# Keys times values ahead of the inverse, and the bonus as 64x64 products, in a chunked RWKV-7 scan

## The chip, the cores and the metric

The kernel runs on one core of one Trainium2 chip. The metric is device time in microseconds (us), the median of three executions. A separate execution was profiled; the traces below are of it. The whole program is two transformer blocks with mixture-of-experts layers and, in the second block, an RWKV-7 branch. The change touches only the scan of that branch.

## The reference, cut to what matters

Each of 8 heads holds a 64x64 state S. Going over the tokens (256 context tokens without output, then 1024 with output), forwards in one direction and backwards in a second, the reference does:

```python
def step(S, inp):
    r_t, w_t, kk_t, b_t, k_t, v_t = inp
    sa = jnp.einsum('bhvk,bhk->bhv', S, -kk_t)
    S = S * w_t[:, :, None, :] + sa[..., None] * b_t[:, :, None, :] + v_t[..., None] * k_t[:, :, None, :]
    y = jnp.einsum('bhvk,bhk->bhv', S, r_t) if emit else None
    return S, y
...
bonus = jnp.sum(r * k_sum * r_k.astype(jnp.float32), axis=-1, keepdims=True) * v
```

The kernel does this in chunks of 64 tokens. Within a chunk the dependence of each token on the ones before it becomes a triangular 64x64 matrix, whose inverse is built in five doublings. The state after a chunk is the decayed state before it, plus B^T times U (U is the solved correction), plus K^T times V (keys times values). The bonus is a sum over 64 channels for each token and head.

## The kernel before, in words

**Work units.** `scan` runs four independent streams: direction d (0, 1) times group g (0, 1) of four heads. Each stream goes over 10 tiles of 128 tokens, the first two of which are context tiles that emit nothing. A tile holds two chunks of 64 (cc = 0, 1), which occupy partition halves. There are 40 pieces of work (stream, tile); "a tile" below means one of them. Each stream has its own SBUF buffers (`b`), two PSUM banks (A and B = A + 1) and its own semaphores.

**Order.** Each engine has a generator per stream that issues a part of the tile's work and yields. `take_turns` starts a stream every `LAG = PHASES // 4` turns (25 // 4 = 6), and in each turn lets all live streams issue one phase, stream 0 first and stream 3 last. So the order in each engine's queue is fixed when the program is built, and is the same rotation on all engines. An engine works its queue strictly in that order. A tile has 25 phases.

The phases of a tile before the change, with the lines of the profile:

- 0: TensorE multiplies the decay and rate low-rank weights (L2387, "lora"); ScalarE takes four tanh (L2516) and one affine pass (L2519).
- 1: VectorE's running sum of the log decay (L2606); GpSimd scales the key (L2561). 2: L2610 on VectorE, L2565 on GpSimd; ScalarE's three exponentials (L2524 to L2526).
- 3: VectorE's block of five operations (L2616 to L2621) that ends with `scaled`.
- 4: TensorE's 16 "pairs" products (L2399), which wait for `scaled`; GpSimd's three products (L2569 to L2571).
- 5: VectorE masks the pairs (L2625, 128x1024). 6: TensorE turns two key tensors (L2410, 128x128 transposes) and forms L_k_v (L2415); ScalarE copies both out (L2530, L2533); VectorE starts the inverse (L2632 to L2636).
- 7 to 16: five levels of the inverse, two phases each: x (L2427, masked by VectorE L2642) and m (L2441, or L2443 in the last level; VectorE adds in L2654 and, but for the last level, turns in L2658).
- 17, 18, 19 for the first chunk and 20, 21, 22 for the second: a (L2456, then VectorE Z L2663), u (L2462, then ScalarE's copy L2540), s (L2471 and L2472, then VectorE's new state L2670). GpSimd forms the decayed state (L2581) at 17 and 20.
- 23: the state's part of y (L2482). 24: the rest of y (L2495, L2497) and the bonus (L2500), then VectorE adds the bonus (L2681) and copies or adds y (L2683, L2685), which releases the banks (`tile_done`) for the stream's next tile.

Each fp32 matmul has two records in the profile, a transpose one. So 8 matmuls are x16. Where a wait stands in the code: s forms both products into one PSUM region,

```python
pe.matmul(out, b.tm[C, 0, col:col + 64], b.U[C, slot(par, jj)], start=True, stop=False)
last = pe.matmul(out, b.tm[C, 1, col:col + 64], v_rows(C, t, slice(h * 64, h * 64 + 64)),
                 start=False, stop=True)
```

and the bonus takes two 128x128 weight loads for four columns each (L2500). All other matmuls of the scan but the transposes and lora are 64x64.

Of the kernel before, what the change touches and what calls it, by code (L numbers as in the profile page):

```python
# [19 lines left out]
ALU = mybir.AluOpType  # L20
ACT = mybir.ActivationFunctionType
# [22 lines left out]

PARTS = [(0, 0), (0, 1), (1, 0)]

PHASES = 25


class Stream:  # L50
# [1978 lines left out]
def rwkv(c, h, hc, w_in, conv, vT):  # L2029
# [205 lines left out]
    for n in range(4):  # L2235
        b = Stream()
        b.lw, b.rate, b.F, b.e1, b.e3, b.kd = (c.at(name, 6 + 8 * n + i, [P, 2, P]) for i, name in enumerate((
            "log_decay", "rate", "running_log", "exp_after", "exp_inverse", "key")))
        b.ar = c.at("a_and_r", 12 + 8 * n, [P, 2, 2, P])
        b.bt, b.kt, b.bb, b.kb, b.rk = b.rate, b.e3, b.lw, b.F, b.kd  # L2240
        H = 74 + 12.5 * n if n < 3 else 38
        b.LL = c.at("pairs", H, [P, 2, 2, 2, 2, 64])
        b.M = c.at("inverse", H + 4, [P, 4, 64])
        b.MT = c.at("inverse_turned", H + 5, [P, 4, 64])
        b.X = c.at("below_diagonal", H + 6, [P, 4, 32])
        b.XW = c.at("below_diagonal_wide", WIDE + n, [P, 4, 64])
        b.tm = c.at("b_and_k_rows", H + 6.5, [P, 2, 256])
        b.LKV = c.at("L_k_v", H + 8.5, [P, 4, 64])
        b.Z = c.at("a_state", H + 9.5, [P, 4, 64])
        b.U = b.LKV  # L2250
        b.S = c.at("state", H + 10.5, [P, 3, 2, 64])
        b.SG = c.at("state_decayed", H + 12, [P, 2, 64])
        b.ge = c.at("decay_to_end", 55.25 + n / 32, [P, 4])
        streams.append(b)
# [77 lines left out]
def scan(c, loads, tiles_of, streams, masks, rw, v_rows, y, sc, ka, half, rate_bias, rks, keep, eye, w2, DEC):  # L2332
# [15 lines left out]
    def first_blocks(a, level, d):  # L2348
# [7 lines left out]
    names = ("lora_done", "tanh_done", "log_ready", "running_ready", "exps_ready", "key_scaled", "key_ready", "scaled",  # L2356
             "ends_scaled", "pairs_done", "pairs_masked", "bk_turned", "bk_copied", "lkv_done", "lkv_copied",
             "mt_ready", "m_ready", "x_done", "x_masked", "x_wide_cleared", "m_done", "a_state_done", "z_ready",
             "u_done", "u_ready", "decayed", "s_done", "state_ready", "y_started", "y_done", "tile_done", "state_cleared")
    both = [f"{n}_{i}" for i in range(4) for n in names]  # L2360
    with stage(nc, "dve_step", "tables_loaded", *both) as (block, dve_step, tables_loaded, *sems):
        sem = [dict(zip(names, sems[i * len(names):(i + 1) * len(names)])) for i in range(4)]
# [10 lines left out]
        def _(pe):  # L2373
            pe.wait_ge(tables_loaded, 16 * len(loads))

            def stream(d, g, b, s, A):
                B = A + 1
                order = (0, 1) if d == 0 else (1, 0)
                for i, t in enumerate(tiles_of[d]):
# [38 lines left out]
                    last.then_inc(s["lkv_done"], 1)  # L2418
                    yield
                    pe.wait_ge(s["bk_copied"], i + 1)  # L2420
                    for level in range(5):
                        n = 5 * i + level
                        pe.wait_ge(s["m_ready"], n + 1)
                        for par, jj in HEADS:
                            h4 = slot(par, jj)
                            for cc, C in CH:
                                last = pe.matmul(ps[C, A, h4 * 32:(h4 + 1) * 32], b.LL[C, par, 0, jj, 0, :],  # L2427
                                                 first_blocks(b.M[C, h4], level, d), start=True, stop=True)
                        last.then_inc(s["x_done"], 1)
                        yield  # L2430
                        if n == 4:
                            pe.wait_ge(s["x_wide_cleared"], 1)
                        if level == 0:
                            pe.wait_ge(s["lkv_copied"], i + 1)
                        pe.wait_ge(s["x_masked"], n + 1)
                        pe.wait_ge(s["mt_ready"], n + i + 1)
                        for h4 in range(4):
                            for cc, C in CH:
                                out = ps[C, B, h4 * 32:(h4 + 1) * 32]
                                if level < 4:  # L2440
                                    last = pe.matmul(out, b.MT[C, h4], b.X[C, h4], start=True, stop=True)  # L2441
                                else:
                                    last = pe.matmul(out, b.XW[C, h4], b.MT[C, h4, second_half(d)],  # L2443
                                                     start=True, stop=True)
                        last.then_inc(s["m_done"], 1)
                        yield
# [3 lines left out]
                    for q, cc in enumerate(order):  # L2450
                        C, n = half_of(cc), 2 * i + q
                        if n:
                            pe.wait_ge(s["state_ready"], n)
                        for jj in (0, 1):
                            for par in (0, 1):
                                last = pe.matmul(ps[C, A + par, jj * 64:(jj + 1) * 64], b.ar[half_of(par), jj, 0, C],  # L2456
                                                 b.S[half_of(par), n % 3, jj], start=True, stop=True)
                        last.then_inc(s["a_state_done"], 1)
                        yield
                        pe.wait_ge(s["z_ready"], n + 1)  # L2460
                        for h4 in range(4):
                            last = pe.matmul(ps[C, A + cc, 256 + h4 * 64:256 + (h4 + 1) * 64], b.MT[C, h4], b.Z[C, h4],  # L2462
                                             start=True, stop=True)
                        last.then_inc(s["u_done"], 1)
                        yield
                        pe.wait_ge(s["u_ready"], n + 1)
                        for jj in (0, 1):
                            for par in (0, 1):
                                col, h = (2 * jj + par) * 64, 4 * g + 2 * jj + par
                                out = ps[half_of(par), A + cc, 256 + jj * 64:256 + (jj + 1) * 64]  # L2470
                                pe.matmul(out, b.tm[C, 0, col:col + 64], b.U[C, slot(par, jj)], start=True, stop=False)  # L2471
                                last = pe.matmul(out, b.tm[C, 1, col:col + 64], v_rows(C, t, slice(h * 64, h * 64 + 64)),  # L2472
                                                 start=False, stop=True)
                        last.then_inc(s["s_done"], 1)
                        yield
                    if emit:
                        pe.wait_ge(s["state_ready"], 2 * i + 2)
                        for q, cc in enumerate(order):
                            C = half_of(cc)
                            for jj in (0, 1):  # L2480
                                for par in (0, 1):
                                    last = pe.matmul(ps[C, A + par, 128 + jj * 64:128 + (jj + 1) * 64],  # L2482
                                                     b.ar[half_of(par), jj, 1, C],
                                                     b.S[half_of(par), (2 * i + q) % 3, jj],
                                                     start=(jj == 0), stop=False)
                        last.then_inc(s["y_started"], 1)
                    yield
                    if emit:
                        pe.wait_ge(s["y_started"], sum(1 for x in tiles_of[d][:i + 1] if x >= 2))
                        for jj in (0, 1):  # L2490
                            for par in (0, 1):
                                h = 4 * g + 2 * jj + par
                                for cc, C in CH:
                                    out = ps[C, A + par, 128 + jj * 64:128 + (jj + 1) * 64]
                                    pe.matmul(out, b.LL[C, par, 0, jj, 1, :], b.U[C, slot(par, jj)],  # L2495
                                              start=False, stop=False)
                                    pe.matmul(out, b.LL[C, par, 1, jj, 1, :], v_rows(C, t, slice(h * 64, h * 64 + 64)),  # L2497
                                              start=False, stop=(jj == 1))
                        for jj in (0, 1):
                            last = pe.matmul(ps[:, A, 384:388], b.rk[:, jj], rks[:, 2 * g + jj, 4 * g:4 * g + 4],  # L2500
                                             start=(jj == 0), stop=(jj == 1))
                        last.then_inc(s["y_done"], 1)
                    yield

# [3 lines left out]
        def _(act):  # L2508
            def stream(d, g, b, s, A):
                B = A + 1  # L2510
                for i, t in enumerate(tiles_of[d]):
# [19 lines left out]
                       .then_inc(s["bk_copied"], 1)  # L2531
                    act.wait_ge(s["lkv_done"], i + 1)
                    act.activation(flat(b.LKV), ps[:, B, 0:256], ACT.Copy, scale=-1.0).then_inc(s["lkv_copied"], 1)  # L2533
                    for _ in range(11):
                        yield
                    for q, cc in enumerate((0, 1) if d == 0 else (1, 0)):
# [13 lines left out]
        def _(pool):  # L2550
            def stream(d, g, b, s, A):
# [3 lines left out]
                for i, t in enumerate(tiles_of[d]):  # L2555
# [3 lines left out]
                    for jj in (0, 1):  # L2559
# [10 lines left out]
                    pool.tensor_tensor(halves(b.kb), halves(b.kt), end(b.ge[:]), ALU.mult)  # L2570
                    pool.tensor_tensor(b.rk[:], r_[:, 2 * g:2 * g + 2, tok(t)], b.kd[:], ALU.mult)\  # L2571
                        .then_inc(s["ends_scaled"], 1)
                    for _ in range(13):
                        yield
                    for q, cc in enumerate((0, 1) if d == 0 else (1, 0)):
                        ends = b.ge[:].rearrange("p (j q) -> p j q", q=2)[:, :, cc].unsqueeze(2)\
# [1 line left out]
                        n = 2 * i + q  # L2578
                        if n:
                            pool.wait_ge(s["state_ready"], n)  # L2580
                        pool.tensor_tensor(b.SG[:], b.S[:, n % 3], ends, ALU.mult).then_inc(s["decayed"], 1)  # L2581
                        yield
                        yield
                        yield
# [6 lines left out]
        def _(dve):  # L2591
# [3 lines left out]
            def stream(d, g, b, s, A):  # L2595
# [4 lines left out]
                for i, t in enumerate(tiles_of[d]):  # L2600
# [34 lines left out]
                    dve.wait_ge(s["mt_ready"], 6 * i + 1)  # L2635
                    dve.transpose(flat(b.M), flat(b.MT)).then_inc(s["m_ready"], 1)  # L2636
                    yield
                    for level in range(5):
                        n = 5 * i + level
                        dve.wait_ge(s["x_done"], n + 1)  # L2640
# [34 lines left out]
                    if emit:  # L2675
# [2 lines left out]
                        tile_y = ps[:, A:A + 2, 128:256].rearrange("p a (j e) -> p a j e", e=64)  # L2678
                        bonus = sc[:, row, 4 * g:4 * g + 4]
                        dve.wait_ge(s["y_done"], sum(1 for x in tiles_of[d][:i + 1] if x >= 2))  # L2680
                        step(dve.tensor_tensor(bonus, bonus, ps[:, A, 384:388], ALU.add))  # L2681
                        if i < tiles_of[1 - d].index(t):
                            dve.tensor_copy(out, tile_y).then_inc(s["tile_done"], 1)  # L2683
                        else:
# [119 lines left out]
```

## Time and profile before

| what | value |
|---|---|
| three runs | 4667.0, 4673.45, 4680.64 us (median 4673.45) |
| the profiled execution | 4685.91 us, of which the span of the trace is 4684.1 us |
| mean granted TensorE clock, whole span | 0.926 of full speed |
| the scan in the trace | 3112 to 3681 us from the span's start: 569 us |
| busy in the scan | TensorE 522.8, VectorE 430.1, ScalarE 163.7, GpSimd 184.6 us |

The scan is 12% of the time. The clock column gives the mean granted TensorE clock of a stretch: 1.00 is 2.4 GHz, 0.50 is 1.2 GHz. A timeline merges neighbouring instructions of one line into one row (start, time from first start to last end, count); a bracket gives idle time before it and the instruction that ended it. Durations of matmuls overlap, so the cost of a group is read from its start to the start of the next group.

### The profile page before, as it was taken

How to read it: one execution, taken by the hardware profiler on the slowest of the kernel's cores; microseconds unless marked ns; L12 is line 12 of the kernel's file. 1: busy time of each engine (PE TensorE's matmuls, PEld its weight loads, DVE VectorE, ACT ScalarE, POOL GpSimd, SP SyncE). 2: the span in 40 equal slices, each digit the busy share in tenths (PEclk: the TensorE clock that was granted, in tenths of full speed). 3: DMA queues.
4: the chain of work that ended last, by engine and by line, in shares of the span. 5: the costliest groups of instructions: out<-in, count | busy, mean ns of one | idle time of the engine just before them, and what ended most of it. 6: DMA issues, size and time to landing. Idle time of an engine off the chain costs nothing. (4 is left out here: it accounts for less than half of the span.)

```text
span 4684.1 us, 80619 instructions
## 1 busy us (share of the span) xinstructions
PE 4090.9 (87%) x33798; PEld 3351.7 (72%) x33798; DVE 2731.3 (58%) x4351; ACT 1734.2 (37%) x2825; POOL 331.2 (7%) x419
## 2 busy tenths in 40 slices
PE   6999986997898998699479877889999587999997
PEld 5878864886786667388367766768888466888886
DVE  2347736885675553688546102647787644556556
ACT  2136622774363442377537211223233112222222
POOL 0000000220000000022000000013333001000000
PEclk9999997998999999799789998978999698999998
DMA  2100027995000002799500112000000121111111
GB/s 101 45 10 2 2 107 274 376 392 193 19 2 1 1 1 78 290 371 397 206 20 2 55 63 72 28 13 3 3 4 3 61 109 63 36 54 37 54 46 41
DMA packets 139157, 425.54 MB, mean 91 GB/s; under 512 B 14661, under 2 KB 50381, under 8 KB 114221
## 3 DMA queue, kind: packets, MB, share of 16 engines
q1 hardware_dynamic: 129580, 386.83, 21.4%
q0 software_dynamic: 9216, 33.56, 2.8%
q8 instruction: 269, 4.41, 0.4%
q14 instruction: 92, 0.75, 0.1%
HBM read 370.03 MB, written 50.33 MB: 90 GB/s over the span
## 5 line engine op out<-in xcount | busy, mean ns | idle before, releaser
L557 PE MATMUL psum<-weight_parts,h_parts 128*128 128x512 f32 (+2 forms) x2880 | 601.5, 371 | 45.8 <-DVE weight_parts L703 29.4
L557 PEld LDWEIGHTS psum<-weight_parts,h_parts 128*128 128x128 f32 x2880 | 508.3, 192 | 133.1 <-DVE weight_parts L703 30.5
L1520 DVE TENSOR_TENSOR weight_parts<-weights_raw,weight_parts 128x2048 fp32r<-128x2048 f32 x192 | 431.6, 2288 | 57.2 <-ACT weight_parts L1490 56.4
L911 ACT ACTIVATE scores<-scores,softmax_stats 128x1024 f32<-128x1024 f32 (+2 forms) x288 | 307.9, 1069 | 331.5 <-DVE softmax_stats L956 331.4
L1490 ACT ACTIVATE weight_parts<-weights_raw 128x2048 fp32r<-128x2048 f32 x192 | 360.4, 1919 | 71.3 <-DMA weights_raw<-in_moe_w_up 42.2
L1428 PE MATMUL psum<-weight_parts,picked_parts 128*128 128x512 f32 x1536 | 364.6, 397 | 15.6 <-DVE weight_parts L1520 10.8
L1901 PE MATMUL psum<-h_parts,up_parts 128*128 128x512 f32 x1536 | 355.4, 393 | 11.0 <-DVE up_parts L1976 11.0
L1917 PE MATMUL psum<-down_parts,hidden_parts 128*128 128x512 f32 x1536 | 353.5, 391 | 6.7 <-DVE down_parts L1981 6.7
L703 DVE TENSOR_TENSOR weight_parts<-weights_raw,weight_parts 128x2048 fp32r<-128x2048 f32 (+2 forms) x48 | 100.7, 2098 | 428.2 <-ACT weight_parts L612 428.1
L1428 PEld LDWEIGHTS psum<-weight_parts,picked_parts 128*128 128x128 f32 x1536 | 291.1, 191 | 79.3 <-issue 11.5
L1901 PEld LDWEIGHTS psum<-h_parts,up_parts 128*128 128x128 f32 x1536 | 291.3, 190 | 72.8 <-DVE up_parts L1976 11.8
L1917 PEld LDWEIGHTS psum<-down_parts,hidden_parts 128*128 128x128 f32 x1536 | 290.1, 189 | 67.7 <-DVE down_parts L1981 7.1
L868 PE MATMUL psum<-identity,scores 128*128 128x128 f32 x2096 | 277.4, 281 | 4.9 <-ACT probs_turned L920 3.0
L868 PEld LDWEIGHTS psum<-identity,scores 128*128 128x128 f32 x2096 | 227.7, 142 | 48.0 <-issue 28.4
L612 ACT ACTIVATE weight_parts<-weights_raw 128x2048 fp32r<-128x2048 f32 (+2 forms) x48 | 84.3, 1757 | 428.7 <-PE psum L557 322.6
L956 DVE CUSTOM_DVE_ANT_0 scores<-psum,zero 128x1024 f32<-128x1024 f32 x128 | 151.6, 1222 | 126.4 <-PE psum L853 126.4
L967 DVE COPY probs_turned<-psum 128x512 f32<-128x512 f32 (+1 forms) x272 | 169.0, 621 | 93.9 <-PE psum L868 92.4
L557 PE MATMUL psum<-weight_parts,mix_parts 128*128 128x512 f32 x768 | 184.8, 398 | 19.2 <-DVE mix_parts L718 19.2
L1976 DVE TENSOR_TENSOR up_parts<-up_raw,up_parts 128x2048 fp32r<-128x2048 f32 x16 | 36.7, 2292 | 270.4 <-ACT up_parts L1935 270.4
L1424 PE MATMUL psum<-weight_parts,activated_parts 128*128 128x512 f32 x768 | 185.9, 398 | 3.8 <-DVE activated_parts L1514 3.8
L1997 DVE TENSOR_TENSOR gated_rows<-psum,gate_rows 128x512 f32<-128x512 f32 x256 | 174.9, 683 | 22.4 <-PE psum L1917 21.0
L557 PEld LDWEIGHTS psum<-weight_parts,mix_parts 128*128 128x128 f32 x768 | 144.8, 191 | 49.7 <-DVE weight_parts L703 16.6
(439 smaller groups left out, 7109.1 us busy)
## 6 DMA issues: line engine op xcount, KB each, us to landing
weights_raw<-in_moe_w_gate SPq DMA_DIRECT2D x64, 1024.0 KB, 13.5
weights_raw<-in_moe_w_up SPq DMA_DIRECT2D x64, 1024.0 KB, 13.9
weights_raw<-in_moe_w_down SPq DMA_DIRECT2D x64, 1024.0 KB, 12.7
w_ada<-in_w_ada SPq DMA_DIRECT2D x12, 2048.0 KB, 10.6
up_raw<-in_w_mlp_up SPq DMA_DIRECT2D x16, 1024.0 KB, 7.3
down_raw<-in_w_mlp_down SPq DMA_DIRECT2D x16, 1024.0 KB, 5.0
weights_raw<-in_even_w_in SPq DMA_DIRECT2D x10, 1024.0 KB, 5.1
weights_raw<-in_w_in SPq DMA_DIRECT2D x10, 1024.0 KB, 5.0
```

The source lines that it names most:

```text
L557: last = pe.matmul(ps[:, t, 0:width(n)], cols[:, i, KP * h + k, t * P:(t + 1) * P], part[:, n % 2, j, k, 0:width(n)], start=(h == 0 and m ...
L868: last = pe.transpose(bank[:, (j % 4) * P:(j % 4 + 1) * P], s_b[:, i % 2, a, lead + j * P:lead + (j + 1) * P], c.ident[:])
L911: act.activation(s_b[:, i % 2, a, 0:w], s_b[:, i % 2, a, 0:w], ACT.Exp, bias=st[:, i % 4, 0, a:a + 1], scale=-1.0, accum_out=st[:, i % 4, ...
L956: dve.tensor_tensor_reduce(s_b[:, i % 2, a, lead:lead + w.width], S_(a)[:, w.col:w.col + w.width], w.bias, -scale, first, ALU.add, ALU.min ...
L967: dve.tensor_copy(pt_b[:, a, 4:m, :].rearrange("p a b -> p (a b)"), ps[:, 4 + g % 3, 0:(m - 4) * P]).then_inc(dve_turned, 1)
L1424: last = pe.matmul(ps[:, 5 + half, :], aT[:, a, 2 * h + k], w[:, b, 2 * k + half], start=(first and k == 0), stop=(final and k == 1))
L1428: last = pe.matmul(ps[:, 2 if kind == "gate" else 3, :], xT[:, a, 4 * h + k], w[:, b, k], start=(first and k == 0), stop=(final and k == 3))
L1490: act.activation(part[:, n % PART_SLOTS, 0], raw[:, n % RAW_SLOTS], ACT.Copy).then_inc(high, 1)
L1520: dve.tensor_tensor(part[:, n % PART_SLOTS, 1], raw[:, n % RAW_SLOTS], part[:, n % PART_SLOTS, 0].bitcast(F32), ALU.subtract).then_inc(low, 1)
L1901: last = pe.matmul(ps[:, i, :], up[:, a, k, f * P:(f + 1) * P], h[:, b, k, half * 512:(half + 1) * 512], start=(n == 0 and k == 0), stop=( ...
L1917: last = pe.matmul(ps[:, 4 + i % 4, :], hidden[:, a, k, t * P:(t + 1) * P], down[:, b, k, half * 512:(half + 1) * 512], start=(n == 0 and ...
L1997: dve.tensor_tensor(gated[:, u % 4], ps[:, 4 + i % 4, :], gate[:, cols], ALU.mult)\
```

## The change

The order of work and two sets of products change. The products of the two chunks' keys and values are made in a phase of their own, after the transposes and ahead of the inverse, into the PSUM columns 256 to 384 of banks A and A + 1; ScalarE copies them to SBUF (`KV`, in the space of the running log decay), and GpSimd adds them to the decayed state in a second operation. The matmul of s then has U only. The bonus becomes eight 64x64 products with one column each, in the phase of the state's part of y, and two small additions on VectorE. TensorE's wait for `lkv_copied` moves ahead of the new products, and it waits for `kv_copied` before the first level. A tile has 26 phases instead of 25; `LAG` stays 26 // 4 = 6.

```diff
-PHASES = 25
+PHASES = 26
...
+        b.KV = b.F
...
                     pe.wait_ge(s["bk_copied"], i + 1)
+                    pe.wait_ge(s["lkv_copied"], i + 1)
+                    for jj in (0, 1):
+                        for par in (0, 1):
+                            col, h = (2 * jj + par) * 64, 4 * g + 2 * jj + par
+                            for cc, C in CH:
+                                last = pe.matmul(ps[half_of(par), A + cc, 256 + jj * 64:256 + (jj + 1) * 64],
+                                                 b.tm[C, 1, col:col + 64], v_rows(C, t, slice(h * 64, h * 64 + 64)),
+                                                 start=True, stop=True)
+                    last.then_inc(s["kv_done"], 1)
+                    yield
+                    pe.wait_ge(s["kv_copied"], i + 1)
                     for level in range(5):
...
-                        if level == 0:
-                            pe.wait_ge(s["lkv_copied"], i + 1)
...
-                                col, h = (2 * jj + par) * 64, 4 * g + 2 * jj + par
-                                out = ps[half_of(par), A + cc, 256 + jj * 64:256 + (jj + 1) * 64]
-                                pe.matmul(out, b.tm[C, 0, col:col + 64], b.U[C, slot(par, jj)], start=True, stop=False)
-                                last = pe.matmul(out, b.tm[C, 1, col:col + 64], v_rows(C, t, slice(h * 64, h * 64 + 64)),
-                                                 start=False, stop=True)
+                                col = (2 * jj + par) * 64
+                                last = pe.matmul(ps[half_of(par), A + cc, 256 + jj * 64:256 + (jj + 1) * 64],
+                                                 b.tm[C, 0, col:col + 64], b.U[C, slot(par, jj)], start=True, stop=True)
...
+                        for jj in (0, 1):
+                            for cc, C in CH:
+                                for par in (0, 1):
+                                    n = 2 * jj + par
+                                    last = pe.matmul(ps[C, A + par, 384 + n:385 + n], b.rk[half_of(par), jj, C],
+                                                     rks[half_of(par), 2 * g + jj, 4 * g + n:4 * g + n + 1],
+                                                     start=False, stop=False)
                         last.then_inc(s["y_started"], 1)
...
-                        for jj in (0, 1):
-                            last = pe.matmul(ps[:, A, 384:388], b.rk[:, jj], rks[:, 2 * g + jj, 4 * g:4 * g + 4],
-                                             start=(jj == 0), stop=(jj == 1))
                         last.then_inc(s["y_done"], 1)
...
                     act.activation(flat(b.LKV), ps[:, B, 0:256], ACT.Copy, scale=-1.0).then_inc(s["lkv_copied"], 1)
+                    yield
+                    act.wait_ge(s["kv_done"], i + 1)
+                    act.activation(b.KV[:], ps[:, A:A + 2, 256:384], ACT.Copy).then_inc(s["kv_copied"], 1)
...
-                    for _ in range(13):
+                    for _ in range(14):
...
-                        pool.tensor_tensor(b.SG[:], b.S[:, n % 3], ends, ALU.mult).then_inc(s["decayed"], 1)
+                        pool.wait_ge(s["kv_copied"], i + 1)
+                        pool.tensor_tensor(b.SG[:], b.S[:, n % 3], ends, ALU.mult).then_inc(s["faded"], 1)
+                        pool.wait_ge(s["faded"], n + 1)
+                        pool.tensor_tensor(b.SG[:], b.SG[:], b.KV[:, cc].rearrange("p (j n) -> p j n", j=2), ALU.add)\
+                            .then_inc(s["decayed"], 1)
...
                     dve.transpose(flat(b.M), flat(b.MT)).then_inc(s["m_ready"], 1)
+                    yield
                     yield
...
-                        step(dve.tensor_tensor(bonus, bonus, ps[:, A, 384:388], ALU.add))
+                        step(*[dve.tensor_tensor(bonus[:, par::2], bonus[:, par::2], ps[:, A + par, 384 + par:388:2],
+                                                 ALU.add) for par in (0, 1)])
```

## Rows read from the trace of the kernel before

**Rows 1.** Busy us (counts) of PE, PEld, DVE, ACT, POOL; clock, DMA; three stretches.
```profile
3112.00:3681.00 569.00, 522.79 (x13024) 489.48 (x13024) 430.06 (x1224) 163.65 (x480) 184.57 (x326) 0.90 0.01 3
...
3457.80:3510.30 52.50, 48.87 (x1344) 45.87 (x1344) 43.33 (x126) 16.37 (x48) 18.42 (x32) 1.00 0.02 4
...
3430.00:3433.00 3.00, 2.96 (x69) 2.96 (x70) 1.27 (x5) 0.00 (x0) 2.22 (x4) 0.54 0.00 0
```

**Rows 2.** Waits in 3300 to 3600: total us, times, longest.
```profile
PE psum L2399 <- DVE exp_inverse L2621: 12.7, 21, 0.6
```

**Rows 3.** Timeline of GpSimd: the first operation released by `scaled`.
```profile
3430.06 0.61 POOL L2569 TENSOR_TENSOR log_decay<-rate,decay_to_end 128x256 f32<-128x256 f32 x1 [3.12 <-DVE exp_inverse L2621]
3444.87 0.61 POOL L2569 TENSOR_TENSOR log_decay<-rate,decay_to_end 128x256 f32<-128x256 f32 x1 [3.13 <-DVE exp_inverse L2621]
3457.88 0.61 POOL L2569 TENSOR_TENSOR log_decay<-rate,decay_to_end 128x256 f32<-128x256 f32 x1 [2.94 <-DVE exp_inverse L2621]
...
3510.34 0.61 POOL L2569 TENSOR_TENSOR log_decay<-rate,decay_to_end 128x256 f32<-128x256 f32 x1 [2.93 <-DVE exp_inverse L2621]
```

**Rows 4.** Timeline of TensorE, one tile's interval from pairs to pairs.
```profile
3470.81 0.67 PE L2399 MATMUL psum<-a_and_r,rate 64*64 64x128 f32 x16 [0.60 <-DVE exp_inverse L2621]
...
3471.75 0.46 PE L2482 MATMUL psum<-state,a_and_r 64*64 64x64 f32 x16
3472.04 0.34 PE L2456 MATMUL psum<-state,a_and_r 64*64 64x64 f32 x5
...
3473.56 0.33 PE L2497 MATMUL psum<-v_rows,pairs 64*64 64x64 f32 x4
3473.82 0.61 PE L2500 MATMUL psum<-r_k_heads,key 128*128 128x4 f32 x4
3474.36 0.62 PE L2462 MATMUL psum<-a_state,inverse_turned 64*64 64x64 f32 x7
...
3476.60 0.71 PE L2387 MATMUL psum<-rwkv_cols,lora_weights 32*128 32x128 f32 x8
3477.25 0.34 PE L2471 MATMUL psum<-L_k_v,b_and_k_rows 64*64 64x64 f32 x4
...
3477.76 0.89 PE L2427 MATMUL psum<-inverse,pairs 64*64 64x32 f32 x25
...
3480.29 0.50 PE L2462 MATMUL psum<-a_state,inverse_turned 64*64 64x64 f32 x5 [0.35 <-DVE a_state L2663]
...
3484.10 0.45 PE L2399 MATMUL psum<-a_and_r,rate 64*64 64x128 f32 x8 [0.60 <-DVE exp_inverse L2621]
```

**Rows 5.** Timeline of VectorE in the same interval.
```profile
3473.14 1.21 DVE L2625 TENSOR_TENSOR pairs<-psum,order_masks 128x1024 f32<-128x1024 f32 x1
...
3478.88 0.29 DVE L2642 TENSOR_TENSOR below_diagonal<-psum,level_masks 128x128 f32<-128x128 f32 x1 [0.17 <-PE psum L2427]
3479.09 0.68 DVE L2606 TENSOR_TENSOR_SCAN running_log<-chunk_starts,log_decay 128x256 f32<-128x256 f32 x1
...
3480.26 0.29 DVE L2654 TENSOR_TENSOR inverse<-inverse,psum 128x128 f32<-128x128 f32 x1
...
3480.96 0.25 DVE L2654 TENSOR_TENSOR inverse<-inverse,psum 128x128 f32<-128x128 f32 x1
...
3483.62 0.42 DVE L2621 TENSOR_TENSOR exp_inverse<-key,exp_inverse 128x256 f32<-128x256 f32 x1
```

**Rows 6.** Timeline of ScalarE in the same interval.
```profile
3476.72 0.38 ACT L2533 ACTIVATE L_k_v<-psum 128x256 f32<-128x256 f32 x1
3477.37 0.62 ACT L2516 ACTIVATE log_decay<-psum,half_biases 128x128 f32<-128x128 f32 x2 [0.26 <-PE psum L2387]
...
3478.38 0.52 ACT L2519 ACTIVATE log_decay<-log_decay,log_rate_bias 128x256 f32<-128x256 f32 x1
```

**Rows 7.** Timeline of GpSimd in the same interval.
```profile
3478.61 1.34 POOL L2561 TENSOR_SCALAR key<-rate,k_a_vectors 128x128 f32<-128x128 f32 x2 [5.55 <-ACT rate L2516]
3479.92 0.40 POOL L2581 TENSOR_TENSOR state_decayed<-state,decay_to_end 128x128 f32<-128x128 f32 x1
```

More of the change, by code:

```diff
@@ L2358, in scan @@
              "mt_ready", "m_ready", "x_done", "x_masked", "x_wide_cleared", "m_done", "a_state_done", "z_ready",
-             "u_done", "u_ready", "decayed", "s_done", "state_ready", "y_started", "y_done", "tile_done", "state_cleared")
+             "u_done", "u_ready", "kv_done", "kv_copied", "faded", "decayed", "s_done", "state_ready", "y_started", "y_done", "tile_done", "state_cleared")
     both = [f"{n}_{i}" for i in range(4) for n in names]
@@ L2496, in stream @@
                                               start=False, stop=False)
-                                    pe.matmul(out, b.LL[C, par, 1, jj, 1, :], v_rows(C, t, slice(h * 64, h * 64 + 64)),
+                                    last = pe.matmul(out, b.LL[C, par, 1, jj, 1, :], v_rows(C, t, slice(h * 64, h * 64 + 64)),
                                               start=False, stop=(jj == 1))
-                        for jj in (0, 1):
-                            last = pe.matmul(ps[:, A, 384:388], b.rk[:, jj], rks[:, 2 * g + jj, 4 * g:4 * g + 4],
-                                             start=(jj == 0), stop=(jj == 1))
                         last.then_inc(s["y_done"], 1)
```

## The prediction

> **What bounds the kernel now.** I read the busy time by stretch first. In the scan TensorE is busy 523 of 569 us, VectorE 430, at a mean granted clock of 0.90; in four undisturbed tiles (52.5 us) TensorE has 48.9, VectorE 43.3, ScalarE 16.4 and GpSimd 18.4 [rows 1]. So TensorE leads, with VectorE close. GpSimd's timeline gives the step: four tiles take 3510.34 - 3457.88 = 52.46 us, 13.12 each [rows 3]. The waits show that TensorE stands 0.60 us ahead of the pairs in every tile (12.7 us, 21 times), for the end of VectorE's block of phase 3 [rows 2]. The timelines of one interval show why. Call the start of the pairs 0 (3470.81). TensorE then works without a stop: the last y product starts at about 2.85, the bonus at 3.01, u at 3.55, lora at 5.79, s at 6.44, x from 6.9 [rows 4]. At 8.07 VectorE masks the last x, at 8.28 it starts the running sum, and then has work without a gap until the block ends at 13.2 [rows 5]. So each tile is 8 us of TensorE and then 5 us of VectorE, in which TensorE has slack (0.35 ahead of u, 0.60 ahead of the pairs). Work taken from TensorE counts only in the first part. Which work stands in which part is set by the rotation, and that is what the new phase alters.
>
> **The change part by part.** The sum is made against the profiled execution (4685.9 us, span 4684.1) and its difference is put on the median, 4673.45, which lies 12.5 us (0.27%) below.
>
> *Bonus.* From the last y product (2.85) to u (3.55) are 0.70 us [rows 4]: two mode changes and four 128-wide records. Without it u would follow one step of about 0.03 later, so 0.66 goes. Eight 64x64 products are added. No row has N=1; the nearest are L2482's eight, which alternate partition halves as these do: 3471.75 to about 3472.04, 0.29 [rows 4]. The other end is s: 3477.25 to 3477.76, 0.51 for eight products [rows 4]. Taken 0.30, the same alternation: -0.36 per emitting tile, between -0.15 and -0.37, in TensorE's part. VectorE's second addition is at most 0.16, the whole of such an operation; y's addition is followed by a wait for TensorE, so I take 0.1 hidden there.
>
> The Trainium skill, TensorEngine Tiling (Array Packing), Instruction Overhead, says that a product with free dimension 1 takes as long as one with 60, about 60 cycles each. By it 16 records would be 16 x 25 ns = 0.40 us at 2.4 GHz, as an estimate, and the gain 0.26; it speaks against splitting two products into eight, but not enough to turn the sign. No run here has N=1 yet.
>
> *Keys times values.* s has 0.51 us for eight products; half goes twice in a tile, -0.26 each. The eight new ones alternate row halves: 0.30 as L2482, up to 0.51 as s. TensorE's work so changes by -0.22 to 0. But s of the second chunk stands in VectorE's part, where its removal only lengthens the 0.60 wait, at a gain of 0.
>
> *ScalarE.* The copy has the shape of L2533: 0.38 us [rows 6]. TensorE's level 0 waits for it, and everything queued behind on TensorE with it. ScalarE handles lora's tanh (3477.37) to the affine pass (3478.38 + 0.52 = 3478.90), 1.65 us after lora's end at 3477.25 [rows 4, 6]. Where that stands ahead of the copy, level 0 can't start until about 2.1 us after lora's end.
>
> *GpSimd.* A second 128x128 operation, 0.40 as L2581 [rows 7], plus a wait, so 0.45 twice a tile: 18.4 + 3.6 = 22.0 of 52.5 us busy [rows 1]. Its new wait for `kv_copied` is met ten phases earlier; behind its wait for its own first operation stands at most L2565, whose product is due in the block 3 us later. The state's sum on VectorE is due two phases (4 us) after the decay. Hidden: 0. If its cover were gone it would cost at most 0.45 x 80 = 36 us.
>
> *The phase.* Number the places of the rotation: phase p of a tile that starts at place T is at T + 4p, since four streams take turns. Starts with 25 phases and lag 6 are T = 0, 25, 50, 75, 100: perfectly even, each tile meets its neighbours alike. With 26 phases the streams still start 25 apart, but a stream's next tile starts 104 after its last: 0, 25, 50, 75, 104. So three tiles come 25 apart and every fourth 29, and the inverse and the chunks are one phase later against the preparation (phases 7 to 25 after: new products, x and m of five levels, a, u, s, a, u, s, L2482 with the bonus, y). Place by place, for TensorE's order from one pairs to the next, with durations from the rows (x, m and u 0.53 each, turn with L_k_v 1.2, lora 0.64, VectorE's m 0.70 [0.25 to 0.29 plus turn, rows 5], block 1.6, pairs' mask 1.21), the four intervals become:
>
> 1. T = 0 to 25: pairs, L2482, a, x, y, u, m, turn, lora, s, x, new products, a, m, x, u, x, m, s, m, x. Neighbours as before up to lora, whose end moves from 6.44 to 6.08 (bonus). Log ready at 7.73, running sum at 7.8 instead of 8.28. Behind it Z, m, x0's mask, L2610, x4's mask; m of level 0 waits for the late x0 (copy at 8.2), x0, u, x4, m: done at 10.3, so VectorE has it at 11.2, block to 12.8. 12.9, that is -0.2.
> 2. T = 25 to 50: pairs, L2482, a, m, y, u, x, turn, lora, s, m, new products, a, x, x, u, m, m, s, x, x. Now m of level 1, not x of level 2, is ahead of the pairs' mask on VectorE: mask done at 4.4, turn 0.2 later than TensorE could (m ends at 2.3, VectorE's add and turn at 3.2, then the mask's 1.21). Two m (1.4) rather than x masks stand right ahead of the block: 13.2, +0.1.
> 3. T = 50 to 75: pairs, L2482, m, m, y, a, x, turn, lora, u, m, new products, s, x, x, a, m, m, u, x, x. Pairs' mask done at 4.7, lora's end 6.6. Now u stands behind lora (place 180 against 179), so ScalarE copies U only after the tanh and the pass: 6.6 + 1.65 + 0.38. s waits to 8.7, x, x, m, m follow to 11.3, VectorE's two m to 12.3, block 13.9: +0.85.
> 4. T = 75 to 104: pairs, s, m, m, L2482, a, x, turn, y, u, m, new products, lora, s, x, x, then as in 1. Four more places between pairs and pairs: s, two m and the new products lie in TensorE's part, and the turn waits for the mask (0.5 more): lora ends at 8.6, running sum at 10.3, then 4.8: 15.1, +2.0.
>
> Sum: -0.2 + 0.1 + 0.85 + 2.0 = +2.75 us in four tiles, 55.2 instead of 52.5. There are nine such rounds between the filling and the emptying of the rotation (40 tiles less four), so +25 us; the 8 context tiles lack the bonus's gain, within the rounding. 4673.45 + 25 = 4698 (profiled 4711).
>
> **The rivals.**
>
> *A. TensorE's work alone decides.* For: 93% busy [rows 1]. Then the sum is -0.36 x 32 - 0.22 x 40 = -20 us: 4653. Against: the 0.60 wait in each tile [rows 2], and removed work in VectorE's part yields nothing. It decides if VectorE and ScalarE slip ahead enough that the longer fourth interval hands back slack to the other three.
>
> *B. Gains and the uneven fourth interval cancel.* If the fourth costs half of what I have (1.0) and the third 0.3, the sum is +1.2 x 9 = +11: 4684, no change that can be told.
>
> *C. GpSimd and VectorE block each other.* The extra additions, 0.40 x 80 = 32 us, would hold VectorE's operations that read two SBUF operands; those in VectorE's part count, say half, +16 on top: 4714. Against: VectorE's running sum, with two SBUF inputs, starts at 3479.09 and takes 0.68 while GpSimd's L2561 runs from 3478.61 to 3479.95 [rows 5, 7]. The Trainium skill, SBUF — State Buffer, "SBUF: two separate sides", calls the shared pair an exclusive lock on which the loser fully blocks; this row shows both at work at once, so the trace does not bear it out here.
>
> *D. The clock.* It falls to 0.54 right behind the 0.60 wait in some tiles [rows 1], and an interval with such a fall is 3444.87 - 3430.06 = 14.81 instead of 13.12 [rows 3], +1.7. The mean of 0.90 says that falls are there throughout. Longer waits could double them: eight more are +14, 4712; fewer would give the like back.
>
> **How the numbers follow.** Chances: forecast 0.50, A 0.22, B 0.13, C 0.05, D 0.10. What this kernel's measurement can tell from no change is 0.3%, 14 us: under 4659 is faster, over 4687 slower. A gives 0.19 faster and 0.03 same; the forecast 0.45 slower, 0.05 same; B 0.10 same, 0.03 faster; C and D slower, but for 0.03 same and 0.01 faster of a steadier clock. Together 0.23, 0.21, 0.56. The likeliest case alone spans 4686 to 4712. The range takes in A's end (4653 less 1) and D's with products at 0.51: 4652 to 4722.
>
> **What would show it.** Right: starts of L2569 in GpSimd's timeline come in a pattern of four with one interval near 15 us and one near 14; ScalarE copies U right behind the affine pass in one tile of four; TensorE waits for `kv_copied` ahead of level 0; the wait ahead of the pairs grows to about 1 us; the gap of the bonus is gone. Wrong: four even intervals below 13.1 us (A), VectorE's operations of unchanged shape getting longer (C), or a mean clock in the scan far from 0.90 with intervals otherwise as before (D).

## The result: 2.2% slower, about four times the forecast loss

The changed kernel takes 4772.9 us (4769.9 to 4782.4, four runs) against 4670.8 before; ratio 1.0221, 95% interval 1.0207 to 1.0235. The forecast was 4698, within 4652 to 4722. The profiled execution of it took 4769.9 us (span 4767.5), 83.4 us more of span than the profiled execution of before, which at 4685.91 us lies above all its timed runs.

Busy time by stretch, columns as in [rows 1]: the scan of the changed kernel, its last regular four tiles, and ten microseconds in them.

```profile
3112.00:3763.00 651.00, 578.52 (x13396) 540.66 (x13398) 433.72 (x1253) 174.94 (x520) 222.66 (x406) 0.76 0.01 3
3499.80:3561.20 61.40, 53.92 (x1393) 50.41 (x1393) 43.68 (x129) 17.44 (x52) 22.40 (x40) 0.86 0.01 3
3527.00:3537.00 10.00, 8.67 (x166) 8.28 (x162) 6.00 (x20) 0.00 (x0) 2.67 (x5) 0.53 0.01 3
```

The scan is 651 us instead of 569: all of the loss is in it. VectorE's busy time is what it was (434, before 430) and GpSimd has 38 us more (forecast 36), but the mean granted clock went from 0.90 to 0.76. Four tiles take 61.4 us, before 52.46 [rows 3], forecast 55.2.

GpSimd's first operation released by `scaled` gives the intervals (L2584 is L2569 of before):

```profile
3423.48 0.61 POOL L2584 TENSOR_TENSOR log_decay<-rate,decay_to_end 128x256 f32<-128x256 f32 x1 [3.19 <-DVE exp_inverse L2640]
3438.39 0.61 POOL L2584 TENSOR_TENSOR log_decay<-rate,decay_to_end 128x256 f32<-128x256 f32 x1 [2.51 <-DVE exp_inverse L2640]
...
3499.82 0.61 POOL L2584 TENSOR_TENSOR log_decay<-rate,decay_to_end 128x256 f32<-128x256 f32 x1 [2.51 <-DVE exp_inverse L2640]
3514.01 0.61 POOL L2584 TENSOR_TENSOR log_decay<-rate,decay_to_end 128x256 f32<-128x256 f32 x1 [2.28 <-DVE exp_inverse L2640]
3528.62 0.61 POOL L2584 TENSOR_TENSOR log_decay<-rate,decay_to_end 128x256 f32<-128x256 f32 x1 [2.56 <-DVE exp_inverse L2640]
3546.31 0.61 POOL L2584 TENSOR_TENSOR log_decay<-rate,decay_to_end 128x256 f32<-128x256 f32 x1 [3.18 <-DVE exp_inverse L2640]
3561.22 0.61 POOL L2584 TENSOR_TENSOR log_decay<-rate,decay_to_end 128x256 f32<-128x256 f32 x1 [2.51 <-DVE exp_inverse L2640]
```

The differences repeat in fours: 14.19, 14.61, 17.69, 14.91. The fourth is the long gap of the rotation, forecast as 15.1. TensorE's timeline in the third, and the pairs that begin the fourth:

```profile
3528.60 1.13 PE L2400 MATMUL psum<-a_and_r,rate 64*64 64x128 f32 x16 [1.33 <-DVE exp_inverse L2640]
3529.51 1.08 PE L2400 MATMUL psum<-a_and_r,exp_inverse 64*64 64x128 f32 x16
3530.38 0.71 PE L2490 MATMUL psum<-state,a_and_r 64*64 64x64 f32 x16
3530.80 0.60 PE L2498 MATMUL psum<-r_k_heads,key 64*64 64x1 f32 x16
...
3540.63 0.38 PE L2480 MATMUL psum<-L_k_v,b_and_k_rows 64*64 64x64 f32 x5 [0.58 <-ACT L_k_v L2555]
...
3546.29 0.67 PE L2400 MATMUL psum<-a_and_r,rate 64*64 64x128 f32 x16 [1.33 <-DVE exp_inverse L2640]
```

TensorE stands 1.33 us ahead of the pairs, not 0.60. In the stretch that begins in this wait the clock is 0.53, and the pairs take 1.78 us (3528.60 to 3530.38) where they took 0.94 [rows 4]. Then s stands 0.58 us for ScalarE's copy of U, behind the tanh, as forecast.

The wait alone doesn't bring the clock down. The pairs at 3546.29 stand behind the same 1.33 us, and the clock stays full:

```profile
3546.30:3561.20 14.90, 12.63 (x389) 11.84 (x389) 11.53 (x35) 4.48 (x13) 5.46 (x10) 1.00 0.02 4
```

The waits ahead of the pairs of one round are 0.60, 1.22, 1.33 and 1.33 us; the clock is low in the first three intervals and not in the fourth, and so in each of the rounds that follow.

### The profile page after: what moved, and what is told of

Its sections match the earlier page's. It is cut to its first block and busy times, and to the rows that moved or that the text cites. A ratio compares the mean times of both kernels' runs of the same rounds, so it can differ in the third digit from the quotient of the medians.

```text
span 4767.5 us, 81658 instructions
## 1 busy us (share of the span) xinstructions
PE 4143.3 (87%) x34182; PEld 3400.5 (71%) x34182; DVE 2735.8 (57%) x4383; ACT 1745.7 (37%) x2865; POOL 369.3 (8%) x499
## 5 line engine op out<-in xcount | busy, mean ns | idle before, releaser
L1520 DVE TENSOR_TENSOR weight_parts<-weights_raw,weight_parts 128x2048 fp32r<-128x2048 f32 x192 | 431.7, 2288 | 57.0 <-ACT weight_parts L1490 55.2
## 6 DMA issues: line engine op xcount, KB each, us to landing
weights_raw<-in_moe_w_gate SPq DMA_DIRECT2D x64, 1024.0 KB, 13.6
```

Of the source, the lines that this page charges most:

```text
L1520: dve.tensor_tensor(part[:, n % PART_SLOTS, 1], raw[:, n % RAW_SLOTS], part[:, n % PART_SLOTS, 0].bitcast(F32), ALU.subtract).then_inc(low, 1)
```

## The experiments

Each time is a median; "before" beside them was 4673 to 4675. "Clock" is the mean granted clock over the scan, to about 0.01. In all of them the scan is where the time differs.

**1. The empty phase alone.** To the kernel before:

```diff
-PHASES = 25
+PHASES = 26
+                    yield   # ahead of level 0, on TensorE, ScalarE, GpSimd and VectorE
```

> The kernel before with one empty phase between the transposes and level 0 of the inverse (26 phases, lag 6), and nothing else. Uneven rotation (streams start 25 places apart, a stream's next tile 29 behind the last start; the waits so opened let the clock fall): most of the loss of the change, 4730 to 4790 us, and GpSimd's starts of L2569 in a pattern of four unequal intervals. Added work (products, copy, GpSimd's addition) as the cause: 4670 +- 10. Each phase costs the same share of the scan: 569/25 = 23 us more, 4694.

Measured: 4776.1 us, ratio 1.0235 (1.0203 to 1.0267), clock 0.77. A loss of the same size is there with none of the added work, and without the bonus's gain (experiment 3). A cost of one phase in 25, 23 us, is far too small. But the loss doesn't lie where the change has it. Late intervals here are 13.07, 13.48, 14.98 and 19.84 us (sum 61.4), so it is the fourth that is long, in the change the first three. And here the waits of 1.23 us leave the pairs behind them fast (0.67 us), while the slow ones (1.13 us) have no wait ahead of them:

```profile
3589.72 0.67 PE L2399 MATMUL psum<-a_and_r,rate 64*64 64x128 f32 x16 [1.23 <-DVE exp_inverse L2622]
...
3604.64 1.13 PE L2399 MATMUL psum<-a_and_r,rate 64*64 64x128 f32 x16
```

So the equal totals are in part a coincidence: the two kernels lose the clock at different places.

**2. All of the change's work in 25 phases.** To the changed kernel; a sketch of TensorE's new order, not the code:

```diff
 x of level 1 (bank A)
+    K^T V of the second chunk into bank A + 1; ScalarE copies its 128 columns
 m of level 1 (waits for that copy)
+    K^T V of the first chunk into bank A; ScalarE copies its 128 columns
 x of level 2 (waits for that copy)
```

> All products, copies and additions of the change, but with 25 phases: the keys times values of the second chunk stand behind x of level 1 and those of the first behind m of level 1, each with a copy of 128 columns, where TensorE had its wait of 0.60 us ahead of the pairs. Uneven rotation as the cause: no loss is left, and per tile 0.36 of the bonus and 0.26 of the first s go from TensorE's part: 4645 to 4662. Added work as the cause: 4730 or more. VectorE and GpSimd locking each other: at least +16, 4687 or more.

Measured: 4668.8 us, ratio 0.9996 (0.9983 to 1.0010), clock 0.88. The loss is gone, and with it the theory of added work (4730 or more) and that of GpSimd and VectorE blocking each other (4687 or more). The time is also above the 4645 to 4662 expected of the order of work: from its fourteenth interval on each is 13.54 to 13.75 us with a fall of the clock in it; the two ahead of that are 12.57 and 12.53.

**3. The bonus alone**, products and two additions as in the change, nothing else:

> The kernel before with the change's bonus alone (eight 64x64 products in the phase of the state's part of y, two additions on VectorE), 25 phases. By the forecast's term: -0.36 x 32 = -11 us, 4659. If the second addition or the small products cost what they save: 4671.

Measured: 4656.9 us, ratio 0.9971 (0.9958 to 0.9984), clock 0.95. Four undisturbed intervals are 12.71, 12.56, 12.52, 12.79 = 50.58 us against 52.46 [rows 3]: 0.47 per tile, forecast 0.36. TensorE's timeline shows the eight products cost even less than assumed:

```profile
3510.34 0.40 PE L2482 MATMUL psum<-state,a_and_r 64*64 64x64 f32 x14
3510.57 0.17 PE L2490 MATMUL psum<-r_k_heads,key 64*64 64x1 f32 x1
...
3510.60 0.32 PE L2490 MATMUL psum<-r_k_heads,key 64*64 64x1 f32 x12
...
3510.79 0.19 PE L2490 MATMUL psum<-r_k_heads,key 64*64 64x1 f32 x1
```

Sixteen records start within 0.22 us, some 15 ns apart, or 29 ns for each product of two records. The Trainium skill's 60 cycles for each matmul (TensorEngine Tiling (Array Packing), Instruction Overhead) are 25 ns at 2.4 GHz, as an estimate. Counted per record, as the prediction did, they are too many; counted per product the trace agrees with them. The eight 64-column products of [rows 4] already had 16 records in 0.29 us, 18 ns each.

**4. An even rotation with more phases.** Four yields at the end of each tile on every engine, `PHASES = 29`, so lag 7:

> The kernel before with four empty phases at the end of each tile: 29 phases, lag 7, so that starts are 29 places apart and even again. Uneven rotation as the cause: near before, 4660 to 4700. Each phase costs the same share: 4 x 23 = 91 us more, 4762. If it is the neighbours' distance rather than evenness that decides, anything in between.

Measured: 4987.4 us, ratio 1.0661 (1.0635 to 1.0687), clock 0.54. A miss of both theories: the rotation is even, and the loss is three times that of the change. Most of its late intervals are 22.9 us. Busy time in nearly the whole scan, which ends at 3990:

```profile
3112.00:3960.00 848.00, 775.17 (x12601) 730.36 (x12605) 431.06 (x1196) 162.38 (x476) 173.47 (x323) 0.54 0.01 3
```

VectorE is busy 431 us in these 848, as before in 569; TensorE shows 775 us busy with nearly all of the same products, at half speed for most of the time. So unevenness is not needed. What 1 and 4 share is a thinner rotation and a clock that falls.

**5. Useless work in the wait.** If the clock is the cause and not a companion, work that serves nothing but to fill TensorE's wait should save time. To the changed kernel, 16 products (n = 4):

```diff
+                    pe.wait_ge(s["tanh_done"], 4 * i + 4)
+                    for _ in range(n):
+                        for cc, C in CH:
+                            for par in (0, 1):
+                                pe.matmul(ps[C, A + par, 256:320], eye[half_of(par), :], eye[half_of(par), :],
+                                          start=True, stop=True)
                     pe.wait_ge(s["scaled"], i + 1)
```

> The changed kernel, and ahead of TensorE's wait for the block of VectorE (phase 4) 16 useless 64x64 products of the identity with itself into a free part of the stream's banks: more work, only to keep TensorE occupied in the wait. The clock as the cause of most of the loss: it falls less often, mean clock in the scan well above 0.76, time 20 to 60 us below the changed kernel's 4773. Only the order of work as the cause, and the clock nothing: no change, or up to 16 x 0.035 x 40 = +20 us more.

Measured: 4706.0 us, ratio to before 1.0064 (1.0046 to 1.0082), clock 0.90: 67 us less with 640 more products. The timelines of GpSimd (L2590 is L2569 of before) and TensorE:

```profile
3504.84 0.61 POOL L2590 TENSOR_TENSOR log_decay<-rate,decay_to_end 128x256 f32<-128x256 f32 x1 [3.18 <-DVE exp_inverse L2646]
3519.75 0.61 POOL L2590 TENSOR_TENSOR log_decay<-rate,decay_to_end 128x256 f32<-128x256 f32 x1 [2.50 <-DVE exp_inverse L2646]
3532.39 0.61 POOL L2590 TENSOR_TENSOR log_decay<-rate,decay_to_end 128x256 f32<-128x256 f32 x1 [2.27 <-DVE exp_inverse L2646]
3545.48 0.61 POOL L2590 TENSOR_TENSOR log_decay<-rate,decay_to_end 128x256 f32<-128x256 f32 x1 [2.56 <-DVE exp_inverse L2646]
3559.52 0.61 POOL L2590 TENSOR_TENSOR log_decay<-rate,decay_to_end 128x256 f32<-128x256 f32 x1 [3.18 <-DVE exp_inverse L2646]
```

```profile
3543.96 0.67 PE L2398 MATMUL psum<-chunk_identity 64*64 64x64 f32 x30
3545.46 0.67 PE L2406 MATMUL psum<-a_and_r,rate 64*64 64x128 f32 x16 [0.84 <-DVE exp_inverse L2646]
3545.95 0.62 PE L2406 MATMUL psum<-a_and_r,exp_inverse 64*64 64x128 f32 x16
```

The useless products leave 0.84 of the 1.33 us wait, the pairs are back at 0.93, and the intervals are 12.64, 13.09, 14.04 and, first in the list, 14.91: 54.7 us. The clock is full in all four:

```profile
3504.80:3559.50 54.70, 48.69 (x1521) 45.22 (x1521) 43.58 (x129) 17.46 (x52) 22.45 (x40) 1.00 0.02 4
```

The changed kernel has 61.4, so 6.7 us of its four tiles are the clock. The fourth interval, in which its clock never fell, is 14.91 in both.

**6. The same in the kernel before (12 products) and with the bonus (12 and 20).**

> The kernel before with 12 such useless products at the same place, in the wait of 0.60 us. The clock as a cost already of the kernel before (its scan has a mean of 0.90): 5 to 20 us faster than 4671. The clock as nothing: same, or up to 10 us slower where the products don't fit into the wait.

> The kernel before with the change's bonus alone (4657) and 12 useless products. If its two to four falls of the clock are avoided: 4645 to 4655, the best of all. If the clock is nothing: 4657 to 4667.

> The bonus alone with 20 useless products instead of 12 (4637). The wait of 0.60 us holds some 20 records of 0.03; 40 records don't fit: if they land on the path, up to +0.6 x 40 = +24, 4640 to 4660; if they only replace waiting at places that the clock needs, 4632 to 4640.

Measured: before with 12, 4655.4 (ratio 0.9960, 0.9945 to 0.9976), clock 0.96; the bonus with 12, **4636.7 (0.9917, 0.9899 to 0.9935)**, clock 0.97, the best of all; with 20, 4643.5 (0.9937, 0.9921 to 0.9954). So the kernel before lost at least some 18 us in its scan to the clock too. With twenty the time is 7 us longer than with twelve, and four intervals of 13.1 to 13.4 appear.

**7. The limits of the filling.**

> The kernel with 29 even phases (four empty ones at the end of a tile, intervals of 22.9 us at a clock of 0.54) and 32 useless products at the same place. The clock as the cause: intervals of 17 us or less wherever the clock holds, hundreds of us less than 4987. The distance of the neighbours alone as the cause: 4987 or more.

> The change's work in 25 phases (4669, with a fall of the clock in each of its last 26 intervals: 13.6 us where 12.5 stand without a fall) and 12 useless products ahead of the pairs. If the falls are all that separates it from the bonus alone: intervals of 12.5, time as the bonus with 12 useless products, 4632 to 4642; keys times values ahead then neither gain nor cost. If the split products themselves hold up TensorE: intervals stay near 13.6, 4660 to 4670.

> The changed kernel with 32 useless products instead of 16. If more occupation takes away further falls (those left in its first half with 16): 4690 to 4705. If the wait of 1.33 us is already full with 16 and the rest lands on the path of the two shorter intervals: 4706 to 4725.

> The empty phase alone (4776) with the 16 useless products of the filled changed kernel (4706). If the order of work costs what it costs there, whatever the added work: by the four intervals with a held clock, 54.7 of the filled changed kernel plus 4 x 0.43 for the bonus that is back = 56.4, so 4706 + 14 = 4720. If the change's own products and copies cost anything with the clock held: below 4706.

Measured: 29 phases with 32, 4858.6 (-129, not the hundreds expected), clock 0.74. Its late intervals go from 15.0 to 22.8 us: the same tiles take 15 us where the clock holds and over 22 where it is mostly low. One of each:

```profile
3786.80:3801.80 15.00, 13.45 (x400) 12.53 (x400) 10.77 (x32) 4.10 (x12) 4.86 (x8) 1.00 0.02 5
3695.70:3718.00 22.30, 21.27 (x403) 20.26 (x400) 11.02 (x31) 4.10 (x12) 4.04 (x9) 0.58 0.01 2
```

At a full clock the 29 phases, with the useless products in them, thus take about 2 us a tile more than the 25 (15.1 against 13.1), 78 us in 39 intervals by this estimate. That is near the 91 us of "each phase costs the same share" in experiment 4; the rest of its 314 us would then be the clock.

 The change's work in 25 phases with 12, 4665.7 (0.9977, 0.9965 to 0.9989), clock 0.90: half of the late intervals return to 12.5 to 12.65, most of the others stay near 13.9. The time is in the range of the rival, but its condition, intervals that stay near 13.6, is met only in half; the filler holds the clock only some of the time, and neither expectation is borne out.

 The changed kernel with 32, 4710.4 (1.0078, 1.0062 to 1.0095): no more help than 16.

The empty phase with 16, 4758.9 (1.0177, 1.0154 to 1.0200), clock 0.81: a miss, 39 us above the 4720 expected, with intervals of 20.5 to 21.7 left. Filling one wait doesn't hold the clock in that order of work, and the run doesn't tell what the added work costs on top of the order. It is 53 us slower than the filled changed kernel, which has the change's products as well. The bonus accounts for some 17 us of this (experiment 3). The rest goes with a lower clock, 0.81 against 0.90, so the change's other work also alters where the clock falls; how is open.

## Why the prediction was wrong

*The order of work was right.* With the clock held (experiment 5) the four intervals are:

| interval | forecast | clock held | changed kernel |
|---|---|---|---|
| 1 | 12.9 | 12.64 | 14.19 |
| 2 | 13.2 | 13.09 | 14.61 |
| 3 | 13.95 | 14.04 | 17.69 |
| 4 | 15.1 | 14.91 | 14.91 |
| sum | 55.2 | 54.7 | 61.4 |

The four-interval pattern, ScalarE's copy behind the tanh and the longer wait ahead of the pairs were all seen. The wait for `kv_copied` ahead of level 0 was not, but for one of 1.3 us in the whole scan. That the filled kernel's 4706 is near the forecast 4698 is in part luck: its mean clock is about the 0.90 that the forecast kept, but its falls lie all in the first half of the scan, while the kernel before has some to the end.

*The clock was the failed step.* The forecast's sum put the change of the clock at nothing, without a reason, and gave "eight more falls, +14 us" as rival D, with a chance of 0.10. The price of a fall, 1.7 us, was about right; their number, eight, came from no row, and that a fall can last was not thought of. In the changed kernel the clock falls in three intervals of four: +1.55, +1.52 and, where it stays low for some 10 us, +3.65 us. And in the context part, where tiles have no y, it hardly recovers: in 3197 to 3252 the clock is 0.50, and the first twelve intervals take 201.2 us against 161.7, so 39 of the loss lie in the first third of the scan.

```profile
3197.00:3252.00 55.00, 52.99 (x866) 50.20 (x867) 31.41 (x88) 13.30 (x39) 15.91 (x30) 0.50 0.01 2
```

Experiment 5 shows the clock to be a cause. Why it stays low so long, and what tips it, is not settled. A wait ahead of the pairs doesn't decide it: 1.33 us are followed by a fall in one interval and by none in the next, and in experiment 2 the clock falls in every late interval though no wait of TensorE there is above 0.44 us and none stands ahead of the pairs. That "the waits so opened let the clock fall", as the expectation of experiment 1 has it, is not shown.

*The bonus* gained 0.47 per tile, not 0.36: the small products were mis-sized, 0.22 us against 0.30. Alone it is worth 17 us (4673.7 to 4656.9).

*Keys times values.* Forecast: -0.26 of s in TensorE's part, worth nothing in VectorE's. With the new products in the old wait and 25 phases, the two undisturbed intervals are 12.57 and 12.53, those of the bonus alone 12.65 on average. So some 0.1 us a tile is gained. That the 12 us between 4668.8 and 4656.9 are the falls that the move brings on fits these intervals, but no run with a full clock throughout shows it.

*Rivals.* A (TensorE's work alone decides, 4653) and B (cancelling, 4684) fell with the result. C: the changed kernel's L2599 has a median of 455 ns but a longest of 854, and L2629 383 to 573 where L2610 had 380 to 426, so the two engines do slow each other now and then. But experiment 2 has all of GpSimd's additions, and its undisturbed intervals are no longer than those of the bonus alone. D was right in kind and some five times too small: the time lies 75 us above the forecast, not 14.

The prediction's evidence against C was misread. [rows 7] merges two operations of GpSimd into one row of 1.34 us; the first takes 0.45, and the second, beside VectorE's running sum, this:

```profile
3479.04 0.91 POOL L2561 TENSOR_SCALAR key<-rate,k_a_vectors 128x128 f32<-128x128 f32 x1
```

In the kernel before, 37 of the 80 operations of this line take 0.84 to 0.91 us, each beside a running sum, and the other 43 take 0.45. So GpSimd is held up by VectorE even there, at a place where almost nothing waits for it; the running sum itself takes 0.68 to 0.70 beside it. C failed because VectorE, which counts, is hardly held up in these rows, and not because the two work undisturbed.

## What to carry to other kernels

In a hand-made rotation of streams, first write down at which distance the pieces of work follow each other after the change: one added phase, empty, cost 100 us here. Where TensorE is close to the bound and the granted clock is already seen to fall in some tiles, an estimate at constant clock was a floor here, not a centre, and the clock's case needs the price of a stretch that stays at 1.2 GHz. Such a wait is worth a trial of filling: 12 useless products in a wait of 0.6 us gained 18 to 20 us in two kernels and 16 gained 67 in the changed one, but 3 and 17 us in the last two orders of experiment 7.

## What the runs showed of the hardware

- TensorE's clock was at half (1.2 GHz) behind a wait of 1.33 us at 3528.60 and full behind the same wait at 3546.29. It fell in experiment 2 with no wait above 0.44 us. With 16 useless products ahead of the same pairs it stayed full through four tiles (experiment 5). The length of the wait alone doesn't tell.
- The clock can stay low through nearly a whole scan: 848 us at a mean of 0.54, TensorE shown as 91% busy (experiment 4). Busy share alone doesn't tell it; the clock column does.
- 64x64 fp32 products with one column started 15 ns apart per record, 29 ns per product, where they alternate row halves (experiment 3).
- A 128x128 operation of GpSimd that took 0.45 us alone took 0.84 to 0.91 beside VectorE's running sum, which took 0.68 to 0.70 there (kernel before).
